# Two MoE layers of a decoder trunk: expert results and residual summed in PSUM, and the residual's SBUF tile lent to one gate weight

## The chip, the cores and the metric

The kernel runs on one NeuronCore of one Trainium2 chip. Its engines are TensorE (PE; its weight loads are shown apart as PEld), VectorE (DVE), ScalarE (ACT), GpSimd (POOL) and SyncE (SP), which issues nearly all DMAs. The metric is the device time of one execution in microseconds; lower is better. PSUM has eight banks of 128 partitions x 512 fp32 numbers.

## The reference

The trunk has two layers of fp32 work on 256 tokens of width 1024. Layer 0 mixes by sparse and stick-breaking attention, layer 1 by a gated linear recurrence, and behind each mixer stands a mixture of 32 SwiGLU experts, of which each token takes two out of one group. A last RMS norm ends it.

```python
for layer in range(DEPTH):                       # DEPTH = 2
    hn = rms_norm(h, norm_mix[layer])
    h = h + mixer(hn)                            # attention, then recurrence
    h = h + hier_moe(rms_norm(h, norm_ffn[layer]), ...)
return rms_norm(h, final_norm)

def hier_moe(x, ...):                            # combine: (tokens, 32), two non-zeros a token
    hid = silu(einsum('sd,edf->sef', xs, w_gate)) * einsum('sd,edf->sef', xs, w_up)
    return einsum('sef,efd->sd', hid * cs[..., None], w_down)
```

Each expert has three weights of 1 MiB (gate, up: 1024 x 256; down: 256 x 1024), so a layer's experts bring 96 MiB, of which every byte is read once.

## The kernel before

**Tokens and quads.** The 256 tokens are two row tiles, t = 0 and 1, of 128 partitions. The 32 experts are taken in eight quads of four, n = 0 to 7; an expert has 32 slots, so a quad's gathered tokens fill 128 columns. The residual h lies in SBUF as 128 x 2 x 1024 fp32 (1 MiB).

**One quad.** `place` (DVE) writes a one-hot matrix `slots`. `gather` (PE, L2211 to L2217) multiplies the normalised rows xg by it, giving the quad's tokens transposed, in two banks: contraction parts k = 0 to 3 in bank 0, k = 4 to 7 in bank 1. ACT (L1040) takes the first bank out to `gatheredT` and DVE (L1558) the second, scaling by the norm's gain. `gate_up` (PE, L2224, called by `first_gate_up` for quad 0 and by `later_gate_up` otherwise) writes gate and up of the four experts into four column strips of bank 3; ACT and DVE make silu(gate) x up; `turn_hidden` (L2259) transposes it into bank 4. `down` (L2279) multiplies by the down weights into banks 5 and 6, which ACT (`rows`, L1065) and DVE (`rows`, L1573) copy to `y_rows`. `combine` (L2208) spreads these rows back to the tokens with the shares as weights: four products (half of the width, t) in banks 7, 2, 0, 1, and `add_rows` (DVE, L1549) adds each to h.

**Order.** PE's program for a layer is route; gather(0) in two halves with the first quarter c = 0 of gate_up(0) between them; quarters c = 1 to 3; gather(1); down(0); gate_up(1); then for n = 2 to 7 `body(n)`: gather(n), combine(n-2), turn_hidden(n-1), gate_up(n), down(n-1), turn_shares(n). ACT in its body(n) does gathered(n), turned(n-1), silu(n), rows(n-1), in this order, and DVE's is alike. All engines meet by semaphores, in an order written by hand.

**Weights.** The ring in SBUF has six slots of 2 MiB, `spare` (in the arena) four more. Quads with an even n take their gate and up weights from the ring, odd ones from `spare`; quad 0's come cut by c rather than by expert. SP issues the loads in one row and waits between them:

```python
for e in range(QE):                                  # quad 2, L628
    sp.wait_ge(s["first_used"], 3 * l + e + 1)       # e < 3: quarter e of quad 0 used
    load_gate_up(sp, l, 2, 0, e)                     # gate and up: 1 MiB each
def later_quad(n, q, parity, ended):
    sp.wait_ge(s[f"gate_up{l}"], n - 1)              # the quad two before is done
    for e in range(QE):
        load_gate_up(sp, l, q, parity, e)
    sp.wait_ge(s[f"down{l}"], n - 1)
    load_down(sp, l, ended)
```

So the eight loads of quad 3 wait for gate_up(1), and those of down weights 2, which are behind them in the row, for down(1).

**Ends of the layers.** After combine(7), `norm_by_halves` (ACT, L814) squares h by halves, `norm` (DVE, L1246) scales it, and at the end of layer 0 PE transposes it and starts the recurrence's input products, in three parts each (high x high, low x high, high x low; `three`, L1850 to L1861). `keep_clock` issues products of the identity that nobody reads.

Of the kernel before, what the change touches and what calls it, by code (L numbers as in the profile page):

```python
# [161 lines left out]
def hybrid_trunk(nc, x, norm_mix, norm_ffn, att_w_in, att_w_out, cmp_pe_k, cmp_w1_k, cmp_w2_k, cmp_pe_v,  # L162
# [3 lines left out]
    with ctx:  # L166
# [204 lines left out]

        def rec_turned(part, b):

            return part[:, 4 * (b % 2):4 * (b % 2) + 4, b // 2 * P:(b // 2 + 1) * P]

        def gather_bank(k, first):

            return bank(2) if first and k in (2, 3) else bank(k // 4)
# [55 lines left out]

        gatheredT = xT[:, 0:4, :].rearrange("p k t -> p (k t)").rearrange("p (k c) -> p k c", k=KD)
# [110 lines left out]
        def _(sp):  # L546
# [30 lines left out]
            for l in range(NL):  # L577
# [85 lines left out]
            for t in range(TT):  # L663
                sp.wait_ge(s["xg_done"], 2 * 2 * NL + t + 1)
                sp.dma_start(out[0, t * P:(t + 1) * P, :], xg[:, t, :]).then_inc(s["out_done"], 16)
            sp.wait_ge(s["out_done"], 16 * TT)
# [117 lines left out]
        START, FIRST, ROUTE, NORM = 6, 2, 19, 10  # L784
# [6 lines left out]
        COMBINE_BANKS = (7, 2, 0, 1)  # L791
# [6 lines left out]
        def _(act):  # L798
# [9 lines left out]
            def norm_by_halves(l):  # L808

                v = 2 * l + 2  # L810
                for half in range(2):
                    for t in range(TT):
                        act.wait_ge(s["h_done"], H_NEEDED[v] + 2 * half + t + 1)
                        link(act.activation(square_moe[:, 0:512], h[:, t, half * 512:(half + 1) * 512], ACT.Square,  # L814
# [63 lines left out]
            def xT_half(v, t):  # L878
                act.wait_ge(s["xT_psum"], 4 * v + 2 * t + 1)
                act.activation((x_hi if v in (0, 2) else xT)[:, 0:4, t * P:(t + 1) * P],  # L880
                               bank(2 * t).rearrange("p (k t) -> p k t", k=4), ACT.Copy)\
# [171 lines left out]
            def turned(l, n, last=False):  # L1053
                act.wait_ge(s[f"hid_psum{l}"], n + 1)
                act.activation(hidT, bank(4)[:, 0:FF].rearrange("p (j c) -> p j c", j=KF), ACT.Copy)\
# [4 lines left out]
                act.activation(shareT, bank(4)[:, FF:2 * FF].rearrange("p (t c) -> p t c", t=TT), ACT.Copy)\  # L1060
                    .then_inc(s[f"shareT{l}"], 1)

            def rows(l, n):
                act.wait_ge(s[f"down_front{l}"], n + 1)
                act.activation(y_rows[:, 0:512], bank(5), ACT.Copy).then_inc(s[f"y_front{l}"], 1)  # L1065
# [7 lines left out]
            def experts(l):  # L1073
# [10 lines left out]
                turned(l, NQ * more + NQ - 1, last=True)  # L1084
                rows(l, NQ * more + NQ - 1)
# [32 lines left out]
            act.wait_ge(s["lb_diff"], 1)  # L1118
            act.activation(lbt[:, 0:2, :], lbt[:, 0:2, :], ACT.Exp).then_inc(s["lb_exp"], 1)
# [111 lines left out]
        def _(dve):  # L1231
            link = Chain(dve, s["dve_chain"])

            def norm(v, t):
                dve.wait_ge(s["norm_rstd"], TT * v + t + 1)
                if v == 0:
# [9 lines left out]
                dve.scalar_tensor_tensor(out=xg[:, t, :], in0=h[:, t, :], scalar=norm_rstd[:, v, t:t + 1],  # L1246
                                         in1=gain[:, :], op0=ALU.mult, op1=ALU.mult)\
                    .then_inc(s["xg_done"], 1)

            def xT_half(v, t):  # L1250
                dve.wait_ge(s["xT_psum"], 4 * v + 2 * t + 2)
                dve.tensor_copy((x_hi if v in (0, 2) else xT)[:, 4:8, t * P:(t + 1) * P],  # L1252
                                bank(2 * t + 1).rearrange("p (k t) -> p k t", k=4)).then_inc(s["xT_back"], 1)

            def x_low(v, t):
# [4 lines left out]
                dve.tensor_tensor(x_lo[:, t], psum[:, 2 * t:2 * t + 2, :].rearrange("p b (k c) -> p (b k) c", k=4),  # L1260
# [280 lines left out]
            def add_rows(l, m, done):  # L1541


                dve.wait_ge(s[f"added{l}"], 4 * m + 4)
                for i, b in enumerate(COMBINE_BANKS):
                    half, t = divmod(i, 2)
                    v = h[:, t, half * 512:(half + 1) * 512]
                    dve.wait_ge(s[f"combined{l}"], 4 * m + i + 1)
# [947 lines left out]
```

## Time and profile before

| | us |
|---|---|
| median of 3 runs | 727.35 (727.25 to 728.49) |
| the profiled execution | 729.75 |
| its span, first to last instruction | 728.0 |
| PE busy | 620.7 (85%) |
| DVE busy | 301.0 (41%) |
| ACT busy | 242.6 (33%) |
| DMA, mean rate over the span | 336 GB/s |

Times inside the kernel are counted from the start of the span. The experts of layer 0 lie between about 160 and 365, those of layer 1 between about 516 and 718. The trace merges rows that follow each other: "x16" is the number of records, and an fp32 product of PE has two.

### The profile page before, as it was taken

The page shows a single profiled execution, that of the slowest core. Times are in us where ns is not written, and L with a number is a line of the kernel's source. Part 1 is how long each engine was busy: PE and PEld are TensorE (multiplying, and loading weights), DVE is VectorE, ACT ScalarE, POOL GpSimd, SP SyncE. Part 2 cuts the span into 40 slices and gives each one's busy share as a digit, 9 for nine tenths or more (in the row PEclk, how much of TensorE's full clock was granted, in tenths as well). Part 3 has the DMA queues.
Part 4 walks back from the last instruction along what each step waited for, and adds up shares of the span by engine and source line. Part 5 has one row for each costly group of instructions (what it writes and reads, how often), then busy time and mean ns, then how long its engine had stood idle before and what let it go on. Part 6 is the DMA issues. An engine that isn't in the chain of part 4 may idle for free.

```text
span 728.0 us, 11030 instructions
## 1 busy us (share of the span) xinstructions
PE 620.7 (85%) x4456; PEld 408.3 (56%) x4456; DVE 301.0 (41%) x518; ACT 242.6 (33%) x540; POOL 35.4 (5%) x64
## 2 busy tenths in 40 slices
PE   9998899999998595675989999999999966595685
PEld 7997787786542341323269987887754431341321
DVE  4556787533232211312285698652522330220304
ACT  5525555451211110100157685662511110110112
POOL 3020000000000100000000001060000000000000
PEclk9999999999999897978999999999999998797979
DMA  8969137798999999999996636569999999999993
GB/s 315 240 234 317 75 116 267 284 407 326 393 422 400 405 422 421 420 423 421 408 387 240 228 123 228 172 266 403 398 386 391 415 422 421 421 422 420 423 415 138
DMA packets 59712, 244.52 MB, mean 336 GB/s; under 512 B 4545, under 2 KB 8913, under 8 KB 38930
## 3 DMA queue, kind: packets, MB, share of 16 engines
q1 hardware_dynamic: 58400, 242.33, 85.0%
q0 software_dynamic: 768, 1.40, 1.0%
q8 instruction: 31, 0.51, 0.3%
q10 hardware_dynamic: 498, 0.15, 0.2%
q14 instruction: 15, 0.12, 0.0%
HBM read 242.82 MB, written 1.05 MB: 335 GB/s over the span
## 4 chain that ended last, share of the span: by engine, by line
PE 51%; DMA 33%; SPq 6%; DVE 5%; issue 2%; ACT 2%; DVEq 0%; ACTq 0%
DMA ring<-in_moe_w_down 31%; PE psum L2279 7%; PE psum L1850 6%; PE psum L2224 6%; PE psum L1861 3%; PE psum L1854 3%; SPq L541 3%; PE psum L2217 3%; PE psum L1859 3%; PE psum L1852 3%; DMA ring<-in_att_w_in 3%; PE psum L2359 2%; SPq L508 2%; PE psum L2361 2%; PE psum L2360 2%
## 5 line engine op out<-in xcount | busy, mean ns | idle before, releaser
L2224 PE MATMUL psum<-arena,xT 128*32 128x512 f32 x512 | 66.0, 674 | 34.5 <-DMA arena<-in_moe_w_up 34.5
L1567 DVE TENSOR_TENSOR arena<-psum,arena 128x256 f32<-128x256 f32 x16 | 6.8, 424 | 212.2 <-ACT arena L1051 212.2
L2224 PE MATMUL psum<-ring,xT 128*32 128x512 f32 x512 | 64.6, 659 | 34.7 <-DMA ring<-in_moe_w_up 34.7
L1047 ACT ACTIVATE arena<-psum 128x256 f32<-128x256 f32 x16 | 6.1, 383 | 203.0 <-PE psum L2224 203.0
L2279 PE MATMUL psum<-ring,arena 128*32 128x512 f32 x456 | 60.3, 612 | 13.5 <-DMA ring<-in_moe_w_down 13.5
L2217 PE MATMUL psum<-arena,xg 128*128 128x128 f32 x512 | 62.4, 280 | 0.8 <-DVE arena L1553 0.8
L2217 PEld LDWEIGHTS psum<-arena,xg 128*128 128x128 f32 x512 | 60.3, 196 | 2.7 <-issue 2.7
L2224 PEld LDWEIGHTS psum<-arena,xT 128*32 128x32 f32 x512 | 17.2, 122 | 78.5 <-issue 43.0
L2224 PEld LDWEIGHTS psum<-ring,xT 128*32 128x32 f32 x512 | 16.5, 120 | 75.4 <-issue 39.3
L1850 PE MATMUL psum<-x_hi,w_hi 128*128 128x256 f32 x224 | 56.0, 288 | 2.2 <-DVE x_hi L1252 1.2
L2208 PE MATMUL psum<-xT,arena 128*128 128x512 f32 x128 | 57.7, 594 | 0.0
L1549 DVE TENSOR_TENSOR h<-psum,h 128x512 f32<-128x512 f32 x64 | 44.1, 689 | 9.3 <-PE psum L2208 8.2
L1854 PE MATMUL psum<-x_hi,w_lo 128*128 128x256 f32 x192 | 47.0, 283 | 0.0
L1850 PEld LDWEIGHTS psum<-x_hi,w_hi 128*128 128x128 f32 x224 | 42.7, 191 | 4.1 <-issue 2.3
L2279 PEld LDWEIGHTS psum<-ring,arena 128*32 128x32 f32 x456 | 15.5, 112 | 50.8 <-issue 34.2
L835 ACT ACTIVATE w_hi<-ring 128x1024 fp32r<-128x1024 f32 x32 | 32.6, 1051 | 23.5 <-DMA ring<-in_att_w_in 12.0
L2208 PEld LDWEIGHTS psum<-xT,arena 128*128 128x128 f32 x128 | 23.1, 190 | 24.6 <-issue 24.6
L410 DVE TENSOR_TENSOR w_lo<-ring,w_hi 128x1024 fp32r<-128x1024 f32 x28 | 33.3, 1220 | 8.5 <-ACT w_hi L835 8.5
L1854 PEld LDWEIGHTS psum<-x_hi,w_lo 128*128 128x128 f32 x192 | 36.8, 191 | 0.0
L1861 PE MATMUL psum<-x_lo,w_hi 128*128 128x256 f32 x224 | 31.5, 283 | 0.1
L1558 DVE TENSOR_TENSOR xT<-psum,gain_ffn 128x512 f32<-128x512 f32 x16 | 11.1, 691 | 46.4 <-PE psum L2217 46.4
L1040 ACT ACTIVATE xT<-psum,gain_ffn 128x128 f32<-128x128 f32 x64 | 18.5, 367 | 32.9 <-PE psum L2217 32.9
(341 smaller groups left out, 1044.7 us busy)
## 6 DMA issues: line engine op xcount, KB each, us to landing
ring<-in_moe_w_down SPq DMA_DIRECT2D x54, 1024.0 KB, 20.6
ring<-in_moe_w_gate SPq DMA_DIRECT2D x32, 1024.0 KB, 15.7
ring<-in_moe_w_up SPq DMA_DIRECT2D x32, 1024.0 KB, 17.6
arena<-in_moe_w_gate SPq DMA_DIRECT2D x32, 1024.0 KB, 21.3
arena<-in_moe_w_up SPq DMA_DIRECT2D x32, 1024.0 KB, 23.1
ring<-in_rec_w_in SPq DMA_DIRECT2D x16, 1024.0 KB, 13.9
ring<-in_att_w_in SPq DMA_DIRECT2D x8, 1024.0 KB, 11.4
ring<-in_att_w_out SPq DMA_DIRECT2D x4, 1024.0 KB, 16.6
```

The source lines that it names most:

```text
L410: eng.tensor_tensor(quarter_lo(base, r), quarter(base, r), quarter_hi(r).bitcast(F32), ALU.subtract)\
L541: sp.dma_start(slot.rearrange("p (e j n) -> p e j n", e=2, j=KF)[:, :, j, :], v[j][:, 2 * i:2 * i + 2, :])\
L835: act.activation(quarter_hi(r), quarter(base, r), ACT.Copy).then_inc(s["w_high"], 1)
L1549: dve.tensor_tensor(v, bank(b), v, ALU.add).then_inc(done, 1)
L1850: pe.matmul(dst, a_hi(k), b_hi(k), start=(k == 0), stop=False)
L1852: pe.matmul(dst, a_hi(k), b_lo(k), start=False, stop=False)
L1854: pe.matmul(dst, a_lo(k), b_hi(k), start=False, stop=False)
L1861: last = pe.matmul(dst, a_hi(k), b_lo(k), start=False, stop=(k == KD - 1))
L2208: pe.matmul(bank(b), shareT[:, t, :], y_rows[:, half * 512:(half + 1) * 512], start=True, stop=True).then_inc(s[f"combined{l}"], 1)
L2217: last = pe.matmul(gather_bank(k, first)[:, k % 4 * P:(k % 4 + 1) * P], xg_parts[:, t, k, :], slots[:, t].rearrange("p e c -> p (e c)"), s ...
L2224: return pe.matmul(bank(3)[e * CAP:(e + 1) * CAP, :].rearrange("p (w f) -> p w f", w=2), gatheredT[:, k, e * CAP:(e + 1) * CAP], w, start= ...
L2279: last = pe.matmul(bank(5 + c)[e * CAP:(e + 1) * CAP, :], hidT[:, j, e * CAP:(e + 1) * CAP], down_part(l, kind, e, j)[:, c * 512:(c + 1) * ...
```

## The change

1. Banks 0 to 3 hold the residual through a layer's experts. `start_sums` puts h there by four products with the identity, behind the route's logits; each `combine` adds to them (`start=False`). `add_rows` and its semaphore are gone. The norm behind the layer and the output read the banks; at the end of layer 0 DVE copies the sums back to h (`h_kept`).
2. The other work has four banks left: `gather` and `down` share 4 and 5, `gate_up` has 6, the transposes 7. For that, down(0) waits for both copies of gather(1), each body's gather waits for the copies of `y_rows` out of its banks, and quarters 0 and 1 of gate_up(0) both stand ahead of the second half of gather(0).
3. The gate weight of quad 2's first expert (1 MiB) goes to h's SBUF tile as soon as `sums_started` and `xg_done` allow. `gate_up` of that expert becomes two products of 256 columns.
4. `keep_clock` behind the route falls from 19 products to 4.
5. At the end of a layer the combine goes row tile by row tile, and the last output goes out in three DMAs instead of two. The recurrence's transposes use banks 4 to 7, its lower bounds are computed ahead of the last quad's end, and its first product is ordered high x high, low x high, high x low (`first_three`).

```diff
+                sp.wait_ge(s["xg_done"], TT * (2 * l + 2))
+                sp.wait_ge(s["sums_started"], l + 1)
+                sp.dma_start(h_weights, moe_w_gate[l].rearrange("(q e) (p r) f -> q e p (r f)", e=QE, p=P)[2][0])\
+                    .then_inc(s[f"gate_up_loaded{l}_0"], 16)
...
-                    load_gate_up(sp, l, 2, 0, e)
+                    load_gate_up(sp, l, 2, 0, e, (0, 1) if e else (1,))
...
-        START, FIRST, ROUTE, NORM = 6, 2, 19, 10
+        START, FIRST, ROUTE, NORM = 6, 2, 4, 10
...
-                        link(act.activation(square_moe[:, 0:512], h[:, t, half * 512:(half + 1) * 512], ACT.Square,
+                        link(act.activation(square_moe[:, 0:512], sum_bank(half, t), ACT.Square,
...
-            def add_rows(l, m, done):
-                dve.wait_ge(s[f"added{l}"], 4 * m + 4)
-                for i, b in enumerate(COMBINE_BANKS):
-                    dve.tensor_tensor(v, bank(b), v, ALU.add).then_inc(done, 1)
...
+                    for t in range(TT):
+                        dve.tensor_copy(h[:, t, :], row_sum(t)).then_inc(s["h_kept"], 1)
...
+            def start_sums(l):
+                for half, t in SUM_TILES:
+                    last = pe.matmul(sum_bank(half, t), ident[:, :], h[:, t, half * 512:(half + 1) * 512],
+                                     start=True, stop=False, skip_group_check=True)
+                last.then_inc(s["sums_started"], 1)
...
+                    pe.matmul(sum_bank(half, t), shareT[:, t, :], y_rows[:, half * 512:(half + 1) * 512],
+                              start=False, stop=last, skip_group_check=True)\
...
+                    if busy and k % 4 == 0:
+                        pe.wait_ge(s[f"y_back{l}" if k else f"y_front{l}"], n - 1)
...
+                        if in_h and e == 0:
+                            for i, part in enumerate((lent, w[0][:, 1])):
+                                pe.matmul(bank(GATE_UP)[0:CAP, i * FF:(i + 1) * FF], gatheredT[:, k, 0:CAP],
+                                          part[:, k, :], start=(k == 0 and i == 0), stop=(k == KD - 1),
+                                          skip_group_check=True)
...
-                gather(l, 0, between=lambda: first_gate_up(l, 0), first=True)
-                for c in range(1, KD // 2):
+                gather(l, 0, between=lambda: [first_gate_up(l, c) for c in range(KD // 4)], first=True)
+                for c in range(KD // 4, KD // 2):
                     first_gate_up(l, c)
                 turn_shares(l, 0)
                 gather(l, 1, between=lambda: turn_hidden(l, 0))
+                pe.wait_ge(s[f"gatheredT{l}"], 2 * GATHERED_PARTS)
                 down(l, 0, early=True)
```

How PE's rows stand, at the start of layer 0's experts. L2217 (L2253 after) is the gather, L2224 (L2260) gate and up, L2253 and L2259 (L2296, L2302) transposes, L2279 (L2322) down. Before:

```order
558 L2217 MATMUL psum<-arena,xg 128x128 [waits slots0,route_exp,xg_done]
560 L2224 MATMUL psum<-ring,xT 32x512 [waits first_loaded0,first_front]
561 L2224 MATMUL psum<-ring,xT 32x512 x7
562 L2217 MATMUL psum<-arena,xg 128x128 x8
563 L2224 MATMUL psum<-ring,xT 32x512 [waits first_loaded1,first_front]
565 L2224 MATMUL psum<-ring,xT 32x512 [waits first_loaded2,gatheredT0]
575 L2217 MATMUL psum<-arena,xg 128x128 x8
576 L2279 MATMUL psum<-ring,arena 32x512 [waits down_loaded0,hidT0]
581 L2224 MATMUL psum<-arena,xT 32x512 [waits gate_up_loaded0_1,gatheredT0]
585 L2217 MATMUL psum<-arena,xg 128x128 [waits slots0,added0]
```

And after, in the same place:

```order
559 L2253 MATMUL psum<-arena,xg 128x128 [waits slots0,route_exp,xg_done]
561 L2260 MATMUL psum<-ring,xT 32x512 [waits first_loaded0,first_front]
563 L2260 MATMUL psum<-ring,xT 32x512 [waits first_loaded1,first_front]
564 L2260 MATMUL psum<-ring,xT 32x512 x7
565 L2253 MATMUL psum<-arena,xg 128x128 x8
566 L2260 MATMUL psum<-ring,xT 32x512 [waits first_loaded2,gatheredT0]
576 L2253 MATMUL psum<-arena,xg 128x128 x8
577 L2322 MATMUL psum<-ring,arena 32x512 [waits down_loaded0,hidT0,gatheredT0]
582 L2260 MATMUL psum<-arena,xT 32x512 [waits gate_up_loaded0_1,gatheredT0]
586 L2253 MATMUL psum<-arena,xg 128x128 [waits y_front0,slots0]
588 L2253 MATMUL psum<-arena,xg 128x128 [waits y_back0]
```

The wait for `gatheredT0` that quarter 2 has now comes straight behind the second half of the gather (a quarter of gate_up stood between them), down(0) has one that it did not have, and gather(2) waits for `y_front0`.

SP's row, ahead of quad 2's loads; `xT` is the last half of down weights 0. Before:

```order
37 L514 DMA xT<-in_moe_w_down 128x1024 [waits route_psum]
38 L500 DMA ring<-in_moe_w_gate 128x2048 [waits first_used]
39 L500 DMA ring<-in_moe_w_up 128x2048
```

After:

```order
37 L518 DMA xT<-in_moe_w_down 128x1024 [waits route_psum]
38 L632 DMA h<-in_moe_w_gate 128x2048 [waits sums_started,xg_done]
39 L504 DMA ring<-in_moe_w_up 128x2048 [waits first_used]
40 L504 DMA ring<-in_moe_w_gate 128x2048 [waits first_used]
```

One of quad 2's eight loads no longer stands behind `first_used`.

## Rows read from the trace of the kernel before

**Rows 1.** Page, part 2: busy tenths and rates in 40 slices of 18.2 us.
```profile
PEclk9999999999999897978999999999999998797979
DMA  8969137798999999999996636569999999999993
GB/s 315 240 234 317 75 116 267 284 407 326 393 422 400 405 422 421 420 423 421 408 387 240 228 123 228 172 266 403 398 386 391 415 422 421 421 422 420 423 415 138
```

**Rows 2.** Chain of waits, 165 to 216: start us, us, what (layer 0).
```profile
167.97 3.65 PE psum L2217 x16
171.62 1.85 PE psum L2224 x16
173.47 1.98 PE psum L2217 x16
175.46 5.33 PE psum L2224 x48
...
185.35 3.57 PE psum L2279 x32
188.92 6.87 PE psum L2224 x64
...
196.16 3.57 PE psum L2217 x32
...
210.39 3.48 PE psum L2279 x32
...
215.57 16.11 DMA ring<-in_moe_w_down
```

**Rows 3.** Windows: PE, PEld, DVE, ACT, POOL busy, PEclk, DMA share, GB/s.
```profile
168.00:171.00 3.00, 3.00 (x15) 3.00 (x16) 2.52 (x15) 0.62 (x2) 0.00 (x0) 0.51 1.05 423
171.00:176.00 5.00, 5.00 (x43) 2.90 (x46) 0.58 (x2) 0.62 (x2) 0.00 (x0) 0.95 0.35 109
190.00:196.00 6.00, 6.00 (x59) 1.84 (x52) 0.00 (x0) 0.14 (x1) 0.00 (x0) 1.00 1.01 423
196.00:199.00 3.00, 3.00 (x29) 3.00 (x28) 1.45 (x3) 2.57 (x8) 0.00 (x0) 1.00 0.82 268
200.00:345.00 145.00, 104.34 (x722) 45.94 (x724) 31.30 (x56) 18.71 (x52) 5.86 (x9) 0.87 1.01 417
528.00:530.00 2.00, 2.00 (x20) 1.88 (x24) 0.00 (x0) 0.00 (x0) 0.00 (x0) 1.00 0.55 111
550.00:554.00 4.00, 4.00 (x38) 3.80 (x35) 1.45 (x3) 2.84 (x8) 0.00 (x0) 1.00 0.81 283
```

**Rows 4.** Timeline of SP's queue: start us, us, issues.
```profile
173.53 0.33 SPq L500 DMA_DIRECT2D ring<-in_moe_w_gate  x1
...
196.01 0.35 SPq L500 DMA_DIRECT2D arena<-in_moe_w_gate  x1
...
214.03 1.88 SPq L508 DMA_DIRECT2D ring<-in_moe_w_down  x4
```

**Rows 5.** DMA issues by line: out<-in, queue, count, KB each, us to landing.
```profile
out<-xg SPq DMA_DIRECT2D x2, 512.0 KB, 2.7
```

**Rows 6.** Timeline of all engines, copies behind the gathers and of down(0).
```profile
175.56 0.69 DVE L1558 TENSOR_TENSOR xT<-psum,gain_ffn 128x512 f32<-128x512 f32 x1 [4.39 <-PE psum L2217]
...
185.39 0.69 DVE L1558 TENSOR_TENSOR xT<-psum,gain_ffn 128x512 f32<-128x512 f32 x1 [2.38 <-PE psum L2217]
...
197.04 0.58 ACT L1065 ACTIVATE xT<-psum 128x512 f32<-128x512 f32 x1
```

**Rows 7.** Timeline of all engines, the route's cover and a combine.
```profile
161.26 4.49 PE L1816 MATMUL psum<-ident 128*128 128x128 f32 x38
...
199.57 3.60 PE L2208 MATMUL psum<-xT,arena 128*128 128x512 f32 x8
```

**Rows 8.** The same place in layer 1, chain of waits.
```profile
524.08 2.02 PE psum L2217 x16
```

**Rows 9.** Timeline, end of layer 1.
```profile
718.16 0.69 DVE L1549 TENSOR_TENSOR h<-psum,h 128x512 f32<-128x512 f32 x1 [0.33 <-PE psum L2208]
718.89 0.63 ACT L814 ACTIVATE arena<-h 128x512 f32<-128x512 f32 x1 [2.01 <-DVE h L1549]
...
722.37 2.48 DVE L1246 SCALAR_TENSOR_TENSOR xg<-h,norm_rstd,gain 128x1024 f32<-128x1024 f32 x2 [0.94 <-ACT norm_rstd L826]
...
723.68 1.55 SPq L665 DMA_DIRECT2D out<-xg  x2
```

**Rows 10.** Timeline, end of layer 0's experts and start of the recurrence.
```profile
375.29 2.34 DVE L1260 TENSOR_TENSOR x_lo<-psum,x_hi 128x1024 fp32r<-128x1024 f32 x2
...
378.82 0.39 PE L1850 MATMUL psum<-x_hi,w_hi 128*128 128x256 f32 x1
...
381.80 0.28 PE L1850 MATMUL psum<-x_hi,w_hi 128*128 128x256 f32 x1
```

More of the change, by code:

```diff
@@ L376, in gather_bank @@
         def gather_bank(k, first):
-            return bank(2) if first and k in (2, 3) else bank(k // 4)
+            return bank(GATHER + (k in (2, 3) if first else k // 4))
         def rows_hi(p):
@@ L1064, in rows @@
                 act.wait_ge(s[f"down_front{l}"], n + 1)
[L1065 removed]
+                act.activation(y_rows[:, 0:512], down_bank(0), ACT.Copy).then_inc(s[f"y_front{l}"], 1)
             def body(l, n):
@@ L1617, in experts @@
                 body(l, NQ * more + NQ - 1, NQ - 1, None)
-                add_rows(l, NQ * more + NQ - 2, s[f"added{l}"])
+                if l == 0:
+                    lower_bounds()
                 rows(l, NQ * more + NQ - 1)
-                add_rows(l, NQ * more + NQ - 1, s["h_done"])
                 for t in range(TT):
@@ L2207, in combine, with gather @@
                         pe.wait_ge(s[f"gatheredT{l}"], GATHERED_PARTS * (gathers + 1))
-                    pe.matmul(bank(b), shareT[:, t, :], y_rows[:, half * 512:(half + 1) * 512],
-                              start=True, stop=True).then_inc(s[f"combined{l}"], 1)
-            def gather(l, n, between=None, first=False):
+                    pe.matmul(sum_bank(half, t), shareT[:, t, :], y_rows[:, half * 512:(half + 1) * 512],
+                              start=False, stop=last, skip_group_check=True)\
+                        .then_inc(s["h_done" if last else f"combined{l}"], 1)
+            def gather(l, n, between=None, first=False, busy=False):
                 pe.wait_ge(s[f"slots{l}"], n + 1)
@@ L2286, in body @@
             def body(l, n, parity, early=False):
-                pe.wait_ge(s[f"added{l}"], 4 * n - 4)
-                gather(l, n)
+                gather(l, n, busy=True)
                 combine(l, n - 2, gathers=n)
                 turn_hidden(l, n - 1)
-                later_gate_up(l, n, parity)
+                later_gate_up(l, n, parity, in_h=early)
                 down(l, n - 1, early=early)
@@ L2319, in experts @@
                 turn_hidden(l, end)
-                pe.wait_ge(s[f"added{l}"], 4 * end)
                 combine(l, end - 1)
+                if l == 0:
+                    pe.wait_ge(s["lb_loaded"], 16)
+                    pe.transpose(bank(GATE_UP)[:, 0:2 * RH], lb_rows[0:2 * RH, :], ident[0:2 * RH, 0:2 * RH])\
+                        .then_inc(s["lb_psum"], 1)
                 down(l, end, last_quad=True)
-                pe.wait_ge(s[f"added{l}"], 4 * end + 4)
-                combine(l, end)
+                combine(l, end, last=True)
                 if l == 0:
-                    keep_clock(NORM, 3)
+                    keep_clock(NORM, TURN)
             experts(0)
```

142 lines of the change are left out of this document (82 added, 60 removed).

## The prediction

> **What bounds the kernel now.** I read the page's slices first, then the chain of waits, then the windows where the two don't say the same. In the slices [rows 1] DMA stands at 9 tenths and 400 to 423 GB/s for most of both expert stages; the exact share between 200 and 345 is full, at 417 GB/s [rows 3]. Those stretches are set by bytes, and nothing PE, DVE or ACT does there moves the end. So the 44 us in which DVE adds to h (64 adds of 0.69 us, one of them in [rows 9]) are mostly free already, and removing them gives nothing except at the end of a layer.
>
> The start of each expert stage is different. From 167.97 the chain runs on PE alone: gather(0), quarter 0, the second half of the gather, quarters 1 to 3, then down(0) at 185.35 and gate_up(1) until 195.79 [rows 2]. Beside it DMA stands nearly still from 171 to 176 (109 GB/s, so 5 x (1 - 109/423) = 3.7 us lost), runs full, and dips again from 196 to 199 (268 GB/s, 1.1 us lost) [rows 3]. The second dip is the telling one. It ends when quad 3's eight loads come, and SP issues the first at 196.01 [rows 4], 0.2 us behind the end of gate_up(1), because their slots are those that gate_up(1) reads. By then the loads issued before had just run out. From there the stream stays full: its end is that moment plus the bytes left. **The time of a layer therefore hangs on when PE finishes gate_up(1).** Layer 1 shows the same two dips, 1.5 us at 528 and 1.3 us at 550 [rows 3].
>
> **The lent megabyte.** Its load can go out once start_sums is through, near 165, and then flows into the first dip: 1.05 MB at 423 GB/s fill 2.5 of its 3.7 us. That part will do what it says. But the seven others of quad 2 then also end 2.5 us sooner, SP has only half a down weight left to issue before gate_up(1) ends, and the gap moves from 171 to just ahead of 196. Nothing in PE's chain between 168 and 196 waits for data [rows 2], so I book no gain. The other end, had the stream been what sets the restart, is 2.5 us in layer 0 and at most 1.5 in layer 1, all of the dip there.
>
> **Longer chain on PE.** Two waits of the change fall into it. (a) Quarter 2 needs DVE's copy of the second half of gather(0). Before, that copy (0.69 us from 175.56, the gather having ended at 175.46 [rows 2, 6]) ran under quarter 1. Now quarter 1 stands ahead of the gather and nothing covers the copy: 0.10 in, 0.69, about 0.1 out, 0.9 us. (b) down(0) now writes the banks of gather(1), so it waits for the same copy, 185.39 plus 0.69 [rows 6], that it ran beside: 0.9 us again. Behind PE queue gate_up(1), and behind that SP's eight loads. Bounds for each are 0.7 (the copy alone) and 1.1. So the restart comes 1.8 us later, in each layer.
>
> (c) gather(2) may not write bank 4 until ACT has taken out down(0)'s first half, which ACT does behind silu(1): the copy ends at 197.04 + 0.58 = 197.62 [rows 6], where gather(2) started at about 196.0. That is 1.7 us. (d) Quad 2's first expert takes two products of 256 columns where it had one of 512. Sixteen groups of four strips took 6.87 us, 0.43 a group [rows 2]; if the strips keep running beside each other the split costs one half-step at the start, 0.4 us; if every pair held up the other three it would be 8 x 0.43 = 3.4. I take 0.4, since four strips do overlap in that row. The Trainium skill, "TensorE: Matmul & The Clock Gate", Part 3, says that matmuls on separate tiles of the array overlap, and "PSUM — Partial Sum Buffer", section Engine vs sequencer instructions, that they start in program order. The trace agrees with the first; read strictly, the second would put the split nearer to 3.4 and each layer 3 us higher.
>
> (c) and (d) hold up down(1), and with it SP's loads of down weights 2, issued at 214.03 [rows 4]. They have slack. Quad 3's 8.39 MB, issued from 196.01, flow some 1.5 us later (an output of 0.52 MB lands after 2.7 us, of which 1.2 are its bytes [rows 5]) and last 19.8 us, to 217.3; the down weights flow from 215.5. So 1.8 us of slack against 1.7 + 0.4 = 2.1: 0.3 us of new gap. With the 3.4 it would be 3.3. Later bodies have the same new waits, but there PE waits for data anyway, and the copies run under turn_shares.
>
> Per layer: 0.9 + 0.9 + 0.3 = 2.1 us; two layers: **+4.2**.
>
> **Other edits of the stage.** start_sums is four products like a combine, 3.60 us, and four idents are 4/19 of 4.49, 0.9 [rows 7]: 4.5 against 4.49, under DVE's route in both. No change. The combine costs what it did; `add_rows` was never waited for.
>
> **Ends.** At the end of layer 1 the first add takes 718.16 to 718.85 and the first square starts at 718.89 [rows 9]: reading PSUM saves 0.73. From the first square to the norm of tile 0 are 3.5 us, with three squares between; by row tiles it is two, so that norm starts 1.8 us earlier, but tile 1's only by the 0.7. Tile 1's norm, in halves of 0.69 (an add from PSUM of the same size), ends 0.6 earlier. The last DMA is half as large, up to 0.6 at 423 GB/s; I take half. **-0.9**, bounds -0.5 and -1.3. At the junction the same 0.7 arrives, but then DVE is in the way: norm, two casts, x_low (1.17 each [rows 10]), a split. Following its new row with these durations, quarter 1 of the recurrence, at 378.82 [rows 10], comes about 0.4 earlier: **-0.4**, bounds 0 and -1. The two copies into h (some 1.3 us each) stand ahead of DVE's split 4, which PE needs three quarters of 3.0 us (378.82 to 381.80 [rows 10]) later, so they are covered; uncovered they would cost 2.6.
>
> **Sum.** 4.2 - 0.9 - 0.4 = +2.9. On the profiled execution (729.75; span 728.0 and 1.75 around it) that gives 732.65. It lies 2.4 above the median of the runs, 727.35, on which I put the same difference: **730.3 us**.
>
> **The clock.** From 168 to 171 the granted clock was 0.51, 1.2 GHz instead of 2.4, after two idle gaps of under 1.2 us, and the first gather took 3.65 us; at the same place of layer 1 it took 2.02 [rows 2, 3, 8]. So a fall costs 1.6 us in this chain, and the same gaps can have it or not. The new waits add gaps of 0.9, 0.9 and 1.7 us. The Trainium skill, same page, Part 1, calls the moment of such changes run-variable; the two layers agree.
>
> **Rivals.**
> - *The clock goes the other way*: layer 0's fall is gone, -1.6, giving 728.7, no change. For it: layer 1. Against: PE's busy and idle times up to 168 are as before.
> - *Short waits*: 0.7 each, no new gap: 2 x 1.4 - 1.3 = +1.5, with a better end 728.5.
> - *More than counted*: one more clock fall, or the split in series: +1.6 or 2 x 3.0, giving 732 to 736. For it: the long idle gap ahead of gather(2).
> - *Faster: the stream sets the restart.* If the loads of quad 2 really end behind PE (they tie within 1 us at 196), the lent megabyte brings the restart forward. It decides for this from the point where PE's chain is shorter than the loads by more than the 1.8 us added; then up to 2.5 + 1.5 and the ends, 1.3: -5.3, 722.0. Half of it is 725. Against it: the dip at 196 to 199 is there before the change, so the loads had run out.
> - *The load doesn't come early* (held by `sums_started`): the dip at 171 stays, and the time is the forecast's, since the dip is worth nothing.
>
> **How the numbers follow.** Forecast 0.50 (728.9 to 732.0), more than counted 0.14, clock or short waits 0.19, faster 0.15, load not early 0.02. The range leaves out the upper end of the slow case and the full gain: 725.0 to 734.0. About 0.2%, 1.45 us, is what a measurement can tell from no change. Slower takes the forecast without its lowest 0.03, the two cases beside it: 0.50 - 0.03 + 0.14 + 0.02 = 0.63; same gets 0.19 + 0.03 - 0.01 = 0.21, faster 0.15 + 0.01 = 0.16.
>
> **What would show it.** Right: the dip at 171 shrinks by over 2 us and the one ahead of the restart grows; PE idles some 0.9 us behind DVE's gather copy twice a layer; gate_up(1) ends near 197.6 and SP issues quad 3's loads there; gather(2) waits for ACT. Wrong: the restart at 196 or sooner, a PE chain without these gaps, or a stream that is no longer full between 200 and 345 for another reason.

## The result, and the profile after the change

The changed kernel takes **733.3 us** (median of 6 runs, 731.7 to 736.6) beside 728.4 for the kernel before in the same two sessions: ratio 1.0079, 95% interval 1.0063 to 1.0094. A second group of runs (e1 below) gave 733.3 against 728.8, ratio 1.0060 (1.0037 to 1.0082). So it is slower by 4.4 to 5.7 us, where +2.9 was forecast. The time itself, 733.3, lies inside the stated range of 725.0 to 734.0. The profiled execution took 732.07 (span 730.4); that of before was 729.75 (span 728.0).

The page's slices of the changed kernel, as [rows 1]:

```profile
PEclk9999999999999797887999999999999998887989
DMA  9969138799799999999996545579998999999993
GB/s 326 275 205 327 44 116 302 286 405 399 316 415 391 408 420 422 419 422 423 403 387 219 218 155 191 208 272 400 407 397 335 385 424 420 420 422 422 421 417 147
```

Slice 10 (164 to 183) has risen from 326 to 399 GB/s; slice 11 (183 to 201) has fallen from 393 to 316 and slice 31 (548 to 566) from 391 to 335. The chain of waits of layer 0 (start us, us, what), as [rows 2]; L2253 is the gather, L2260 gate and up, L2322 down, L1582 and L1084 the copies of DVE and ACT:

```profile
166.84 2.02 PE psum L2253 x16
168.86 3.57 PE psum L2260 x32
172.43 2.00 PE psum L2253 x16
174.52 0.70 DVE xT L1582
175.26 3.68 PE psum L2260 x32
...
183.55 0.70 DVE xT L1582
184.30 3.64 PE psum L2322 x32
187.94 6.91 PE psum L2260 x64
...
196.21 0.43 ACT xT L1084
196.78 3.81 PE psum L2253 x32
```

The three new waits stand in it as they were named: (a) DVE's copy behind the second half of gather(0), (b) the same behind gather(1), and (c) ACT's copy ahead of gather(2). The first gather takes 2.02 us where it took 3.65 [rows 2]: in this execution TensorE's granted clock did not fall there.

Windows of the changed kernel (us, busy us of PE, PEld, DVE, ACT, POOL, clock, DMA share, GB/s), to be held against [rows 3]. The first is the place of the old dip behind gather(0); the second the restart of layer 0; the next two the restart and the load of down weights 2 in layer 1:

```profile
169.87:174.87 5.00, 4.54 (x40) 2.38 (x32) 0.50 (x3) 0.00 (x0) 0.00 (x0) 1.00 1.02 401
194.90:197.90 3.00, 1.39 (x12) 1.18 (x12) 1.45 (x3) 1.67 (x4) 0.00 (x0) 1.00 0.57 164
543.00:555.00 12.00, 10.39 (x96) 3.89 (x89) 1.45 (x3) 1.70 (x4) 0.00 (x0) 1.00 0.73 289
569.00:580.00 11.00, 11.00 (x80) 6.60 (x76) 2.89 (x6) 2.98 (x9) 0.58 (x1) 1.00 0.94 359
```

The kernel before, in the last two of them:

```profile
543.00:555.00 12.00, 12.00 (x105) 6.28 (x98) 2.20 (x5) 2.84 (x8) 0.00 (x0) 1.00 0.94 371
569.00:580.00 11.00, 11.00 (x80) 6.14 (x82) 3.76 (x7) 1.80 (x6) 0.22 (x1) 1.00 1.01 410
```

The dip at 171 is filled (401 GB/s, it was 109), and the queue runs dry ahead of the restart instead. SP's issues, as [rows 4]: the lent megabyte, the first of quad 3, down weights 2.

```profile
163.91 0.33 SPq L632 DMA_DIRECT2D h<-in_moe_w_gate  x1
...
195.03 0.35 SPq L504 DMA_DIRECT2D arena<-in_moe_w_gate  x1
...
214.94 1.97 SPq L512 DMA_DIRECT2D ring<-in_moe_w_down  x4
```

**How the executions are compared from here on.** The part ahead of gather(0) of layer 0 ends between 165.1 and 168.0 in the executions profiled, whichever the kernel, so I measure each layer from the start of its gather(0): to the end of gate_up(1) ("PE"), and to the first product of down(7)'s second half, which waits for the last load ("layer"). A + marks a layer whose gather(0) took 2.9 to 3.7 us instead of 2.02, the clock having fallen. "Lost" is the stream lost up to 90 us behind gather(0): over windows of 3 us from 6 us ahead of it, the sum of 3 x (1 - rate/421). "Junction" is from that same product in layer 0 to gather(0) of layer 1, "end" from it in layer 1 to the end of the span.

| kernel | PE 0 / 1 | layer 0 / 1 | lost 0 / 1 | junction | end |
|---|---|---|---|---|---|
| before | 27.75+ / 26.12 | 195.3+ / 191.1 | 6.8 / 3.8 | 160.8 | 12.9 |
| changed | 27.90 / 27.90 | 195.7 / 195.1 | 7.5 / 6.9 | 161.4 | 11.4 |
| e1 changed again | 27.90 / 29.51+ | 195.7 / 196.8+ | 7.5 / 7.8 | 160.2 | 11.4 |
| e2 no lent MB | 27.90 / 27.90 | 197.0 / 193.6 | 7.8 / 6.4 | 160.3 | 11.4 |
| e3 (a), (b) undone | 26.12 / 26.13 | 194.9 / 191.6 | 6.3 / 4.7 | 160.3 | 11.4 |
| e4 (c) undone | 27.90 / 29.49+ | 195.4 / 194.5+ | 7.1 / 7.3 | 161.5 | 11.4 |
| e5 early down weights | 27.90 / 29.49+ | 190.3 / 190.9+ | 2.3 / 2.7 | 160.4 | 11.4 |
| e6 before, early | 27.76+ / 26.13 | 194.2+ / 190.4 | 6.0 / 3.3 | 160.8 | 12.9 |
| e7 before, (a) and (b) | 29.52+ / 29.48+ | 197.3+ / 194.4+ | 8.5 / 7.1 | 161.0 | 12.9 |
| e8 all undone, early | 27.74+ / 26.13 | 192.4+ / 189.5 | 4.4 / 1.7 | 160.2 | 11.4 |
| e9 e5 again | 29.50+ / 27.90 | 192.3+ / 188.3 | 4.1 / 1.2 | 160.4 | 11.4 |
| e10 e5, no lent MB | 27.91 / 27.90 | 191.5 / 189.7 | 3.7 / 2.5 | 160.4 | 11.4 |
| e11 e5, (b), (c) undone | 27.04 / 28.62+ | 190.2 / 190.2+ | 2.3 / 2.7 | 160.4 | 11.4 |
| e12 e11, 6 idents | 27.06 / 27.04 | 189.9 / 188.2 | 2.2 / 1.2 | 160.4 | 11.4 |

"Layer" less "lost" is 187.0 to 189.2 in all rows, while the layers themselves run from 188.2 to 197.3: most of what a layer gains or loses, it gains or loses as stream within 90 us of its first gather. Differences under 2 us between single layers can't be read from this table.

### The profile page after: what moved, and what is told of

Same layout as the page of the kernel before. It is cut to its first block, busy times and chain, and to the rows that moved or that the text cites. A ratio compares the mean times of both kernels' runs of the same rounds, so it can differ in the third digit from the quotient of the medians.

```text
span 730.4 us, 10875 instructions
## 1 busy us (share of the span) xinstructions
PE 619.3 (85%) x4444; PEld 407.0 (56%) x4444; DVE 260.1 (36%) x457; ACT 242.6 (33%) x540; POOL 35.2 (5%) x64
## 4 chain that ended last, share of the span: by engine, by line
PE 54%; DMA 31%; DVE 6%; SPq 5%; ACT 2%; issue 2%; DVEq 0%; POOL 0%; ACTq 0%; POOLq 0%
DMA ring<-in_moe_w_down 31%; PE psum L2322 7%; PE psum L1863 6%; PE psum L2260 5%; PE psum L1874 3%; PE psum L1867 3%; SPq L545 3%; PE psum L1872 3%; PE psum L1865 3%; PE psum L2253 3%; PE psum L2403 2%; PE psum L2404 2%; PE psum L2405 2%; SPq L512 2%; PE psum L2240 1%
## 5 line engine op out<-in xcount | busy, mean ns | idle before, releaser
L2260 PE MATMUL psum<-ring,xT 128*32 128x512 f32 x480 | 65.1, 668 | 36.6 <-DMA ring<-in_moe_w_up 34.9
L2260 PE MATMUL psum<-arena,xT 128*32 128x512 f32 x512 | 64.6, 662 | 34.6 <-DMA arena<-in_moe_w_up 34.6
L2322 PE MATMUL psum<-ring,arena 128*32 128x512 f32 x456 | 60.1, 610 | 14.4 <-DMA ring<-in_moe_w_down 12.8
L2253 PE MATMUL psum<-arena,xg 128*128 128x128 f32 x512 | 60.9, 276 | 4.1 <-ACT xT L1084 3.2
L2253 PEld LDWEIGHTS psum<-arena,xg 128*128 128x128 f32 x512 | 58.7, 192 | 6.3 <-issue 6.3
L2260 PEld LDWEIGHTS psum<-arena,xT 128*32 128x32 f32 x512 | 16.9, 121 | 77.4 <-issue 41.8
L1863 PE MATMUL psum<-x_hi,w_hi 128*128 128x256 f32 x216 | 53.9, 287 | 0.7 <-issue 0.3
L2260 PEld LDWEIGHTS psum<-ring,xT 128*32 128x32 f32 x480 | 15.0, 121 | 69.0 <-DMA ring<-in_moe_w_up 35.6
L1867 PE MATMUL psum<-x_hi,w_lo 128*128 128x256 f32 x184 | 45.1, 283 | 0.0
L2322 PEld LDWEIGHTS psum<-ring,arena 128*32 128x32 f32 x456 | 15.2, 112 | 51.4 <-issue 32.3
L1863 PEld LDWEIGHTS psum<-x_hi,w_hi 128*128 128x128 f32 x216 | 41.2, 191 | 2.4 <-issue 2.0
L1867 PEld LDWEIGHTS psum<-x_hi,w_lo 128*128 128x128 f32 x184 | 35.2, 192 | 0.0
L1582 DVE TENSOR_TENSOR xT<-psum,gain_ffn 128x512 f32<-128x512 f32 x16 | 11.1, 691 | 51.9 <-PE psum L2253 51.9
L1874 PEld LDWEIGHTS psum<-x_lo,w_hi 128*128 128x128 f32 x216 | 27.8, 192 | 0.0
```

What stands on the lines that cost most here:

```text
L1863: pe.matmul(dst, a_hi(k), b_hi(k), start=(k == 0), stop=False)
L1867: pe.matmul(dst, a_lo(k), b_hi(k), start=False, stop=False)
L1874: last = pe.matmul(dst, a_hi(k), b_lo(k), start=False, stop=(k == KD - 1))
L2253: last = pe.matmul(gather_bank(k, first)[:, k % 4 * P:(k % 4 + 1) * P], xg_parts[:, t, k, :], slots[:, t].rearrange("p e c -> p (e c)"), s ...
L2260: return pe.matmul(bank(GATE_UP)[e * CAP:(e + 1) * CAP, :].rearrange("p (w f) -> p w f", w=2), gatheredT[:, k, e * CAP:(e + 1) * CAP], w, ...
L2322: last = pe.matmul(down_bank(c)[e * CAP:(e + 1) * CAP, :], hidT[:, j, e * CAP:(e + 1) * CAP], down_part(l, kind, e, j)[:, c * 512:(c + 1) ...
```

## The experiments

Medians and ratios are to the kernel before, run on the same chip in the same group: e1 to e4 are one group (before 728.77), e5 to e8 the next (727.92), e9 to e12 the last (727.88). Theory T, in the expectations, is the mechanism of the forecast: the load stream restarts when PE ends gate_up(1).

**e1, the changed kernel again.**

> The changed kernel once more, as the yardstick of this group. Theory T (the restart of the load stream hangs on the end of gate_up(1), and the load of down weights 2 on the end of down(1)): from the start of gather(0) to the end of gate_up(1) 28.0 us in both layers; 4.6 to 5.7 us above the kernel before. Rival U (the excess over the forecast was a stray of one execution): 2.9 above.

733.28 us, ratio 1.0060 (1.0037 to 1.0082). The interval is +2.7 to +6.0 us and just reaches the +2.9 of the forecast; that of the first group, +4.6 to +6.8, does not. The excess over the forecast is no stray of one execution.

**e2, without the lent megabyte.**

```
-                sp.dma_start(h_weights, ...[2][0]).then_inc(s[f"gate_up_loaded{l}_0"], 16)
...
-                    load_gate_up(sp, l, 2, 0, e, (0, 1) if e else (1,))
+                    load_gate_up(sp, l, 2, 0, e)
...
-                later_gate_up(l, n, parity, in_h=early)
+                later_gate_up(l, n, parity)
```

> The gate weight of quad 2's first expert is loaded into the ring behind first_used, as before the change, and its products are 512 columns wide again; all else as changed. Theory T: the lent megabyte is worth nothing as long as PE sets the restart: within 0.5 us of the changed kernel, or up to 0.8 below it (the split's 0.1 to 0.4 a layer is gone). The dip at 171 comes back and the one ahead of the restart shrinks by as much. Rival S (the stream sets the restart): 2.5 us later in layer 0 and 1.5 in layer 1, so up to 4 us above the changed kernel.

732.74 us, ratio 1.0062 (1.0040 to 1.0085): as e1. The restart comes at the same 27.90, and by 33 us behind gather(0) the stream lost is 5.4 to 5.5 us with the megabyte and without it. In this kernel it is worth nothing that these runs can tell; their two intervals leave some 2 us, under the 4 of rival S. The two layers differ from those of the changed kernel by +1.3 and -1.5 us, most of it not in "lost" (+0.2 and -0.5) but in how late the last load lands. turn_shares(2) starts 19.94 us behind the end of gate_up(1) with the split products and 19.89 without, so the split costs 0.05 us.

**e3, waits (a) and (b) undone**, the sums still in PSUM.

```
-            return bank(GATHER + (k in (2, 3) if first else k // 4))
+            if second and k >= KD // 2:
+                return bank(GATE_UP)
+            return bank(TURN if first and k > 3 else GATHER + (k in (2, 3) if first else k // 4))
...
-                gather(l, 0, between=lambda: [first_gate_up(l, c) for c in range(KD // 4)], first=True)
-                for c in range(KD // 4, KD // 2):
+                gather(l, 0, between=lambda: [first_gate_up(l, 0), pe.wait_ge(s["passes_ready"], l + 1)], first=True)
+                for c in range(1, KD // 2):
...
-                pe.wait_ge(s[f"gatheredT{l}"], 2 * GATHERED_PARTS)
                 down(l, 0, early=True)
```

> Undoes waits (a) and (b) with the sums still in PSUM: the second half of gather(0) goes to bank 7, so quarter 1 of gate_up(0) stands behind it again; the second half of gather(1) goes to bank 6, which gate_up(1) writes only later, so down(0) need not wait for its copy. Theory T: gate_up(1) ends 26.2 us behind the start of gather(0) instead of 28.0, in both layers, and all behind it moves along: 3.6 us below the changed kernel. Rival S (the loads of quad 2 hold the restart once PE is sooner): under 1.5 us below it.

728.30 us, ratio 0.9996 (0.9982 to 1.0010), 5.0 under e1 where 3.6 was expected; the two intervals together allow it. Its chain of waits in layer 1:

```profile
520.79 2.02 PE psum L2256 x16
522.82 1.85 PE psum L2263 x16
524.67 1.98 PE psum L2256 x16
526.65 5.33 PE psum L2263 x48
...
534.76 1.79 PE psum L2256 x16
536.55 3.57 PE psum L2325 x32
540.12 6.91 PE psum L2263 x64
```

No DVE row stands between PE's: gather, quarter, gather, three quarters, and down(0) straight behind gather(1). PE's stretch is the old 26.13. With it the layers go down by 0.8 and 3.5 us. In layer 0 it is less than PE's 1.8, because between 45 and 90 us behind gather(0) this kernel loses 2.6 us of stream and the changed one 2.2. (a) and (b) are the larger part of the change's price, and neither was necessary for the four banks.

**e4, wait (c) undone.** ACT and DVE each copy the rows of down(0) ahead of silu(1).

```
-                body(l, 1)
+                gathered(l, 1)
+                turned(l, 0)
+                rows(l, 0)
+                silu(l, 1)
...
-                silu(l, 1)
                 rows(l, 0)
+                silu(l, 1)
```

> Undoes wait (c): ACT and DVE copy the rows of down(0) ahead of silu(1) instead of behind it, so that gather(2) finds banks 4 and 5 empty. Theory T, the excess lies in the load of down weights 2, which waits for down(1): gather(2) starts 0.2 us behind gate_up(1) instead of 1.9, down(1) ends 18.1 to 18.3 us behind it instead of 19.9, and the piece of layer 1 in which the stream is under 400 GB/s behind 572 closes: 1.7 to 2.2 us gained in layer 1, 0.4 to 1.7 in layer 0, 2 to 3.9 in all below the changed kernel. By my forecast's own slack of 1.8 us only 0.3 a layer, 0.6 in all. Rival M (the stream dips there for a reason of its own): under 0.5.

729.74 us, ratio 1.0025 (1.0007 to 1.0044), 3.5 under e1 by the medians and 2.6 by the means (730.5 and 733.1): of the 12 runs three took 733.0 to 733.2, with a mean granted clock of 0.937 to 0.939, and the six fastest 728.1 to 729.4, with 0.944 to 0.947. gather(2) starts 0.28 us behind the end of gate_up(1) instead of 2.05, and turn_shares(2) 18.10 instead of 19.94. Between 45 and 90 us behind gather(0) layer 1 loses 0.4 us of stream, where the changed kernel loses 1.5 and the kernel before 0.2. The window of the load of down weights 2 in layer 1, e4:

```profile
571.00:580.00 9.00, 9.00 (x60) 5.86 (x56) 1.71 (x3) 2.30 (x7) 0.58 (x1) 1.00 1.01 398
```

and the changed kernel:

```profile
571.00:580.00 9.00, 9.00 (x60) 5.86 (x56) 1.71 (x3) 2.30 (x7) 0.58 (x1) 1.00 0.93 346
```

398 GB/s against 346 (SP issued the down weights at 571.95 and 571.98, and quad 3's loads at 553.9 in e4 and 552.1 in the changed kernel). So 18.1 us between the two groups of loads keep the stream nearly full and 19.9 don't. The slack that the forecast gave this load is what falls here.

**e5, three of quad 2's four down weights issued behind down(0).** Their slots are free from then on; they used to stand in SP's row behind the waits for gate_up(1) and down(1).

```
-                load_down_half(sp, last_half(l, 0), l, 1, 0, s[f"down_loaded{l}"])
+                load_down_half(sp, last_half(l, 0), l, 1, 0, s["ahead_loaded"])
+                load_down(sp, l, 2, range(QE - 1))
...
+                sp.wait_ge(s[f"down{l}"], 2)
+                load_down(sp, l, 2, (QE - 1,))
```

> The changed kernel, with three of the four down weights of quad 2 (3.1 MB) issued behind down(0), whose slots they take, ahead of quad 3's loads, instead of behind down(1). Theory T (PE is late and the queue runs dry twice, ahead of the restart and at down weights 2): both gaps are filled, and of the 6.6 to 7.0 us of stream that a layer of the changed kernel has lost 60 us behind gather(0) some 1.5 remain: the stretch from gather(0) to the last down is 4 to 5.5 us shorter in each layer, the kernel 8 to 11 us below the changed one, about 723 to 726. PE's chain to gate_up(1) stays at 28.0. Rival P (PE's later program takes the stream's place as the bound once the gaps are filled): 1 to 4 us below the changed one.

**720.49 us**, ratio 0.9902 (0.9883 to 0.9921): 7.4 under the kernel before. e1 was 4.5 above it in its own group, so the move is worth 11.9 us, more than the 8 to 11 that were expected. SP's issues and the windows of restart and down weights 2:

```profile
186.94 2.45 SPq L512 DMA_DIRECT2D ring<-in_moe_w_down  x3
193.44 0.33 SPq L504 DMA_DIRECT2D arena<-in_moe_w_gate  x1
```

```profile
188.00:198.00 10.00, 8.39 (x78) 4.32 (x71) 1.45 (x3) 2.29 (x7) 0.00 (x0) 1.00 1.01 412
213.00:230.00 17.00, 16.20 (x128) 8.72 (x128) 1.71 (x3) 3.00 (x10) 2.10 (x3) 1.00 1.02 408
```

PE's chain is as long as in e1 (27.90, and 29.49 where the clock fell), and the stream is at 412 and 408 through both places. So what the longer chain cost, it cost by letting the queue run dry. The edit also writes out SP's loop over the quads; e6 has the same edit in the kernel before and gains 0.7, so that is not where the 11.9 come from.

**e6, the same move in the kernel before.**

> The same move of three down weights in the kernel before. Theory T: only the gap at the restart (1.1 and 1.3 us) and the shallow one at down weights 2 (0.4 to 0.7) are there to be filled; the dip behind gather(0), 1.5 to 3.7 us, stays, since quad 2's loads wait for first_used. 2.5 to 3.7 us below the kernel before. Rival P: under 1.

727.23 us, ratio 0.9989 (0.9974 to 1.0004): 0.7 under the kernel before, a miss for theory T (2.5 to 3.7) and inside what rival P allowed. The profile gives 1.1 us in layer 0 and 0.7 in layer 1, of which "lost" shows 0.8 and 0.5. The restart is nearly full in layer 0:

```profile
192.00:200.00 8.00, 8.00 (x54) 5.39 (x45) 4.29 (x8) 2.85 (x8) 0.00 (x0) 1.00 1.00 398
522.00:535.00 13.00, 12.83 (x112) 7.14 (x111) 3.44 (x13) 3.36 (x12) 0.00 (x0) 1.00 0.89 342
```

but the second row, the dip behind gather(0) of layer 1, is still there, and with it 2.4 of the 3.3 us that the layer loses. The window ends 14.8 us behind gather(0) and takes in a new dip: 336, 344 and 311 GB/s at 1 us a window from 10 us behind gather(0), where the kernel before had 410, 451 and 426. Why it is there stays open.

**e7, (a) and (b) alone in the kernel before.**

```
-                gather(l, 0, between=lambda: first_gate_up(l, 0), first=True)
-                for c in range(1, KD // 2):
+                gather(l, 0, between=lambda: [first_gate_up(l, c) for c in range(2)], first=True)
+                for c in range(2, KD // 2):
...
+                pe.wait_ge(s[f"gatheredT{l}"], 2 * GATHERED_PARTS)
                 down(l, 0, early=True)
```

> The kernel before with the order of quarters 0 and 1 and the wait ahead of down(0) as in the change, nothing else: (a) and (b) alone. Theory T: gate_up(1) ends 1.8 us later in each layer, 27.9 behind gather(0) instead of 26.1, and each layer is 1.8 longer, 3.6 us above the kernel before; less the 0.4 or so a layer that first_used comes later for quad 2's loads, hidden ahead of the restart. Rival S (the stream hides it): under 1.5.

731.94 us, ratio 1.0053 (1.0033 to 1.0073), +4.0 where 3.6 was expected. Some of it may be the clock: its runs show a mean granted clock of 0.940 against 0.9435. The gaps in its chain of waits are those of the changed kernel:

```profile
172.35 2.00 PE psum L2217 x16
...
174.44 0.70 DVE xT L1558
175.14 0.04 issue
175.19 3.69 PE psum L2224 x32
```

The second half of the gather ends at 174.35 and quarter 2 starts at 175.19: 0.84 us.

**e8, (a), (b), (c) undone and the early loads.** The edits of e3, e4 and e5.

> The changed kernel with (a), (b) and (c) undone and the three down weights early: what both theories leave of the change is the sums in PSUM, the lent megabyte and the ends. Theory T: with the queue never dry PE's chain of 28.0 or 26.1 us makes no difference, so it is within 1 us of e5, about 722 to 725. Rival P: PE's chain still counts, and it is 3 to 5 us below e5.

723.65 us, ratio 0.9947 (0.9928 to 0.9967): 3.2 **above** e5. Neither theory had that. PE's stretch is as short as before, and the time is longer. One difference to e5 is that quarter 1 stands behind the second half of the gather again. The gate weight of quad 2's second expert waits for quarter 1 (`first_used` 2); SP issued it 9.4 us behind gather(0) (176.72), in e11 5.6 (172.80). 1.6 of those 3.8 us are the clock that fell in e8. Layer 1 can be compared without a fall: there e8 issued it 7.8 us behind gather(0) and e12 5.6, and e8 lost 1.8 us of stream by 33 us behind gather(0), e9 and e12 1.1 each; its layer is 1.2 to 1.3 longer than theirs. The windows 5 to 12 us behind gather(0), e8 and then e11:

```profile
172.00:179.00 7.00, 7.00 (x64) 3.19 (x60) 1.45 (x3) 0.00 (x0) 0.00 (x0) 1.00 0.84 294
```

```profile
172.00:179.00 7.00, 6.15 (x56) 2.80 (x48) 1.45 (x3) 0.00 (x0) 0.00 (x0) 1.00 1.01 403
```

**e9, e5 again.**

> The kernel of e5 once more, as the yardstick of this group: about 1% under the kernel before, 720 to 722. From gather(0) of layer 0 to the end of the span 553 us.

720.58 us, ratio 0.9902 (0.9885 to 0.9920).

**e10, e5 without the lent megabyte.** The edits of e2 and e5.

> The kernel of e5 with the lent megabyte taken back (its gate weight loaded into the ring behind first_used, its products 512 wide). Theory T: in the changed kernel the megabyte was worth nothing because the queue ran dry later all the same; now that the queue no longer runs dry, a dip behind gather(0) is final, and the megabyte is worth what it fills: 1.5 us or so in each layer, the kernel 2.5 to 3.5 us above e5, and the stream lost by 60 us behind gather(0) 1.5 larger. Rival N (it is worth nothing anywhere, since the stream catches up): within 0.8 us of e5.

723.40 us, ratio 0.9944 (0.9924 to 0.9964): 2.8 above e9. Layer 1, without a fall of the clock in either, is 1.4 longer and loses 1.3 more. The dip behind gather(0) of layer 1, e9 and then e10:

```profile
522.00:528.00 6.00, 5.15 (x52) 2.63 (x44) 1.43 (x6) 0.14 (x1) 0.00 (x0) 1.00 1.03 397
```

```profile
522.00:528.00 6.00, 5.15 (x48) 2.67 (x44) 1.45 (x3) 0.00 (x0) 0.00 (x0) 1.00 0.78 294
```

The same megabyte was worth nothing in e2 against e1.

**e11, e5 with (b) and (c) undone, the new order of the quarters kept.**

> The kernel of e5 with waits (b) and (c) undone but the new order of the quarters kept. e8, with (a) undone too, was 3 us above e5 where theory T had allowed 1. Theory O (undoing (a) cost it: quarter 1 behind the second half of the gather is used 1.9 us later, and with it goes the load that waits for first_used 2, into a queue that is short there): this kernel is within 1 us of e5, and keeps 400 GB/s or more 3 to 9 us behind gather(0) in layer 0. Rival F (e8 lost to something that (b) and (c) did, or to a clock fall that a shorter wait brings): 2 to 3 us above e5.

720.44 us, ratio 0.9898 (0.9881 to 0.9914), as e9. So it is undoing (a) that costs e8 its 3.2 us. That it costs by the later load, theory O, fits the rates above; but the profiles show no more than 1.3 us a layer of it. That PE is 0.9 us sooner at the restart and 1.8 at down(1) makes no difference that these runs can tell.

**e12, e11 with two more products in `keep_clock` behind the route.**

```
-        START, FIRST, ROUTE, NORM = 6, 2, 4, 10
+        START, FIRST, ROUTE, NORM = 6, 2, 6, 10
```

> The kernel of e11 with 6 products in keep_clock behind the route instead of 4, so that they end near 165.2 when the member products can start, instead of 0.6 us earlier. If the idle of 0.6 us there is what lets the clock fall at gather(0) (3 of 8 looks at the changed order in layer 1 so far), gather(0) takes 2.02 us in both layers and the kernel is 0 to 1.6 us below e11; if the fall comes from elsewhere, as before, with no difference in time.

**719.04 us**, ratio 0.9887 (0.9872 to 0.9902), the fastest kernel here, 1.1% under the kernel before. gather(0) takes 2.02 us in both layers; against e11 the intervals overlap, and one profile does not show that the two extra idents are the reason.

## Why the prediction was off

The forecast had the direction and the mechanism, and the time lies in its range, but it said +2.9 where +4.4 to 5.7 was measured. The step that failed is the slack of down weights 2: waits (c) and (d) were booked at 0.3 us a layer, and they cost 0.6 to 1.3. The two profiled spans differ by only 2.3 us, and it needs the parts to see why: -1.1 ahead of gather(0), +0.4 layer 0, +0.5 junction, +4.0 layer 1, -1.5 end. The first is scatter (165.1 to 168.0 for all kernels). Layer 0 of before had a clock fall that cost PE 1.6 us, and the changed one had none: the rival "the clock goes the other way" came true in this one pair of executions, by luck. Without these two the pair gives 2.3 + 1.1 + 1.6 = +5.0, which is what the runs say. Of the 3.0 us between the forecast of 730.3 and the 733.3 measured, 1.1 are the base: 727.35 was the median of three runs, that of six is 728.4. By steps:

- **gate_up(1) sets the restart: right.** (a) and (b) were put at 0.9 each. PE's stretch grew from 26.12 to 27.90, 1.78 for both, in either layer; e7 adds them alone (+4.0 us in all), e3 takes them away (-5.0). The forecast's 197.6 for the end of gate_up(1) took layer 0's clock fall along; it came at 194.8.
- **The lent megabyte at 0: right for this kernel** (e1 and e2), and for the reason given. It is not a property of the megabyte: e10 puts it at 2.8 us once the queue no longer runs dry. The rival "the stream sets the restart" was wrong here.
- **(c) and (d), "1.8 us of slack against 2.1", so 0.3 a layer: this step failed.** Between 45 and 90 us behind gather(0) the layers of before lose 1.6 and 0.2 us, those of the changed kernel 2.2 and 1.5, of e1 2.2 and 1.2, of e2 2.4 and 1.1: 0.6 to 0.7 in layer 0 and 1.0 to 1.3 in layer 1, together 1.6 to 1.9 where 0.6 was booked. Undoing (c) alone brings layer 1 back to 0.4 (e4). The delay itself was booked high enough: from the first load of quad 3 to the down weights it grew from 18.0 us to 19.9, by 1.9 where 2.1 was taken. The slack was reckoned from the last byte of quad 3 to the first of the down weights, as if the stream ran at full rate up to the one and from the other on. It does not: in layer 1, at 1 us a window, it falls from 418 to 295, 250, 299 GB/s from 49 us behind gather(0), which is where the forecast's reckoning puts the last byte (28.2 + 1.5 + 19.8 = 49.5), and it is back at 426 only eight windows later, although SP issued the four loads from 48.1 to 50.1 us. Whether the tail of quad 3 thins out or the down weights start slowly, the one issued 0.5 us behind the other, these windows don't separate. The Trainium skill, "DMA: Bandwidth & Descriptors", section Queues, rings and completion order, says that each DMA engine has a ring of its own for a queue. That would make a stream thin out engine by engine; no row here shows single engines.
- **(d) itself**: 0.4 was taken, bounds to 3.4; it is 0.05 (e1 and e2). The reading by which the split costs eight half-steps a layer is refuted; whether the products start in program order is not tested by it.
- **Junction: -0.4 forecast.** From the last down of layer 0 to quarter 1 of the recurrence it was 15.57 us before (363.25 to 378.82). In e1 and e2 it is 14.87: -0.7. In the profiled changed kernel it is 16.1: PE idles 1.65 us for x_hi's copy, and then its first two parts run at a granted clock of 0.56 and 0.50. They are in its chain of waits:

```profile
373.33 0.61 DVE x_hi L1273
373.94 0.20 issue
374.14 1.88 PE psum L1880 x8
376.02 1.71 PE psum L1883 x8
377.72 1.02 PE psum L1886 x8
```

  Eight such products start to start took 1.67 and 1.71 us there, and 1.03 and 1.08 in e1 (374.56, 375.59, 376.67):

```profile
374.56 1.18 PE L1880 MATMUL psum<-x_hi,w_hi 128*128 128x256 f32 x8 [1.65 <-DVE x_hi L1273]
375.59 1.17 PE L1883 MATMUL psum<-x_hi,w_lo 128*128 128x256 f32 x8
```

  The same idle gap, and the clock held in e1. Of the ten profiles of the changed kernel and its variants with `ROUTE` 4, the junction is 160.2 to 160.4 in eight; in the two others, the changed kernel and e4, it is 161.4 and 161.5, and both had the first two parts at 1.7 to 1.9 us.
- **End of layer 1: -0.9 forecast, -1.5 measured** (12.9 in the three kernels of the old form, 11.4 in the others), beyond the bound of -1.3. The two output halves land after 2.1 us (the page's DMA issues) where a whole tile took 2.7 [rows 5]: the full 0.6, of which I had booked half.
- **What is left.** Layer 1 of the changed kernel is 4.0 longer: 1.8 by (a) and (b), 1.3 by (c) and (d), and 0.9 that is not in "lost": layer less lost is 188.2 there, 187.2 in e2 and 187.3 before. It is also 188.2 in e5 and 187.1 in e9, which are one kernel, so it is scatter in how raggedly the last loads land, and no part of the change. The runs price the terms higher than the profiles do: 4.0 to 5.0 for (a) and (b) (e7, e3) and 2.6 to 3.5 for (c) (e4). The lower two with -1.5 for the end and -0.6 for the junction make +4.5, so the sum closes with the price that the runs give (c), of which the profiles show 1.2 to 1.6. Why the runs say 4.4 to 5.7 rather than the 3.4 and 4.1 that the profiles of the changed kernel and e1 show from gather(0) of layer 0 onward stays open. How often the clock falls in executions that are not profiled can only be guessed from each run's mean: of the kernel before in e1's group, the six runs with 0.946 took 727.6 us on average and the seven with 0.941 took 729.2, apart by the price of one fall.

## What to carry to other kernels

Where loads wait for the engine that they feed, the question of an edit is not how long the engine's chain grows but whether the queue runs dry while it waits; look in the issuing engine's row for loads whose slots are free long before the wait they stand behind. Here moving three such loads, 3.1 MB, was worth 11.9 us in the changed kernel, more than undoing (a) and (b) (5.0) and undoing (c) (3.5) gave one by one; in the kernel before, which kept its dip behind gather(0), the same move gave 0.7. The megabyte sent early was worth nothing while the queue ran dry after it, and 2.8 us once it didn't; so such edits are to be judged together, not one by one. And slack between two groups of loads is not the gap between their reckoned bytes: here the next group was issued 1.4 us ahead of the reckoned end of the one before it, and the rate was down for 8 us all the same.

## What the runs showed of the chip that I had not expected

- Two products of 256 columns on one strip, beside three strips with one of 512, cost 0.05 us more than four of 512 over a whole gate_up of 6.9 us.
- Where a stream of eight 1 MB loads ends and four more, issued just ahead of its reckoned end, follow, the rate is low for several microseconds: 418, 295, 250, 299, 360 GB/s in windows of 1 us in layer 1 of the changed kernel.
- At gather(0) the granted clock fell in some executions and not in others of the same kernel. In the ten profiles with `ROUTE` 4 it fell twice in layer 0 and four times in layer 1; in the three with 19 (the old form) three times and once; in the one with 6 not at all. Each fall lengthens PE's chain by 1.6 us. In e5 and e9, one kernel, the layers with a fall are 2.0 and 2.5 us longer than those without, although the chain of PE no longer sets the restart: quarter 1 is used later, and the loads of quad 2 with it.
- Undoing a wait made a kernel slower (e8 against e5, +3.2 us; e11 shows that it is wait (a)). The order that brought the wait had also freed a slot 2.1 us earlier; that this is the whole reason is not shown.
